# Making the scores of the dilated attention's next block between turning one block and multiplying another

## The chip, the cores and the metric

The kernel runs on one core of one Trainium2 chip. Its time is the device time of one execution in microseconds (us), the median of several runs. The engines are named as the profile names them: PE is TensorE (PEld its weight loads), DVE is VectorE, ACT is ScalarE, POOL is GpSimd, SP is SyncE. Each engine works through a queue of its own, and the queues meet only at semaphores.

## The reference, cut to what matters

The reference is two transformer blocks one after the other, on 1024 tokens of width 1024. The second block has four mixers side by side. Two of them matter here: an attention over dilated windows, and a state-space mixer called S5.

```python
DIL_PAIRS = ((128, 1), (512, 4), (2048, 16))      # window, dilation: three groups of four heads of 64

def dilated_group(q, k, v, bias_tab, window, dil):
    ...
    s = jnp.einsum('bdhnqe,bdhnke->bdhnqk', qb, kb, preferred_element_type=jnp.float32) / math.sqrt(E)
    s = jnp.where(mask[None, None, None], s + bias[None, None, :, None], -1e30)
    m = jnp.max(s, axis=-1, keepdims=True)
    p = jnp.exp(s - m)
    den = jnp.sum(p, axis=-1, keepdims=True)
    o = jnp.einsum('bdhnqk,bdhnke->bdhnqe', p, vb.astype(jnp.float32)) / den

def s5_mixer(u, a_re, a_im, log_dt, b_re, b_im, c_re, c_im, d_skip, w_glu):
    ...
    bu = jnp.einsum('gpc,bsgc->bsgp', b_bar, uf.astype(jnp.complex64))
    ...
    _, h = lax.associative_scan(combine, (a, bu), axis=1)
    ...
    y = jax.nn.gelu(y.reshape(B_, S_, S5_WIDTH))
    gl = y @ w_glu.astype(f32)
    y = gl[..., :S5_WIDTH] * jax.nn.sigmoid(gl[..., S5_WIDTH:])
```

## The kernel before, in words

The kernel is a sequence of stages with a barrier between them. The stage in question, `pool_and_dilated` (L3358), lies between 2298 and 2560 us of the span. It holds three kinds of work in one list of 45 steps: 6 steps of a pooling mixer, 28 of the dilated attention, 11 that mix its three groups. Every engine walks through the same steps, but each in its own time: the steps only fix the order inside each queue.

The attention has 24 blocks of 128 queries, 8 for each dilation, in the order 4, 16, 1. Block j is spread over several steps. Step 6 + j of each queue holds:

- PE: `scores(j)` (L3463; queries times keys for four heads, into two accumulator banks), `turn(j - 2)` (L3479; transposes the exponentials of block j - 2), `outputs(j - 3)` (L3489; turned exponentials times values).
- DVE: `largest(j)` (L3549; scales the scores and adds the bias, L3558, then takes maxima), `take_turned(j - 2)` (L3567), `output(j - 3)` (L3575, divides).
- ACT: `exps(j - 1)` (L3641), `take_turned(j - 2)` (L3650).

A block sees one or two parts of keys: with dilation 4 the odd blocks have two parts, with 16 all have one, with 1 all but the first have two. Two parts double the matmuls of a block. The profile counts each float32 matmul as two instructions, so `scores` shows as 8 or 16, `turn` as 4 or 8, `outputs` as 8 or 16.

Two waits tie these together. `scores(j)` waits for `scores_read`, which DVE raises in `largest(j - 1)` once it has read the two banks at L3558. `output(j - 3)` on DVE waits for `outputs(j - 3)` on PE.

After these pieces, each step appends others to the same queue. `turn_values` (L3415) transposes four blocks of values on PE; `take_values` (L3425, copy at L3435) empties them on DVE in even steps and on ACT in odd steps. Then one piece of the S5 core (class `S5Core`, L4277) may follow. Its four groups m are put at fixed steps:

```python
core = S5Core(c, io, s5, rooms, yT, (3, 7, 11, 15), (9, 13, 17, 21), (25, 28, 31, 34, 37, 40, 42, 44), u_loaded[1])
```

At steps 3, 7, 11, 15 PE runs `inputs(m)` (L4306); one step later DVE runs `turn(m)` (L4362), two steps later `scan(m)` (L4366 to L4373). POOL then makes the state from the scan (L4420). At steps 9, 13, 17, 21 PE runs `outputs(m)` of the core (L4319 and L4322, 48 instructions), called S5 outputs below. They wait for POOL's state, and for DVE having read the accumulators of the next group:

```python
            pe.wait_ge(self.s_ready, m + 1)
            pe.wait_ge(self.x_made, 4 * min(m + 2, 4))
```

When S5 outputs of group m are done, POOL issues the loads for group m + 1 (L4507, L4509), stores group m (L4439, after ACT's gelu, L4399), fetches the group before (L4444) and makes the state of group m + 1. From step 25 on PE runs eight gate products (L4336, two steps each), which read what POOL stored and fetched (`y_back`). ACT's sigmoid (L4406) and DVE's multiplication (L4380) follow each, and the next product waits for that multiplication.

Of the kernel before, what the change touches and what calls it, by code (L numbers as in the profile page):

```python
# [3357 lines left out]
def pool_and_dilated(c, io, proj, skewed, s5, rooms, heads, yT, spare, ident):  # L3358
# [3 lines left out]
    G, BLOCKS = len(POOLS), 3 * NB  # L3362
# [85 lines left out]
    def side_pe(pe):  # L3448
        for s in range(N_POOL):
            g = s - 1  # L3450
            if 0 <= g < G:
                if g == 0:
                    pe.wait_ge(pool_loaded, 32)
                pe.wait_ge(p_ready, g + 1)
                if g >= 2:
                    pe.wait_ge(p_out, g - 1)
                for n in range(2):
                    last = nc.tensor.matmul(c.ps[:, S0 + 2 * (g % 2) + n, :], wg[:, g, :], pooled[:, g % 2, n * BANK:(n + 1) * BANK],
                                            start=True, stop=True)
                last.then_inc(p_mixed, 1)  # L3460
            yield

        def scores(j):  # L3463
            n, b = divmod(j, NB)
            qk, (mine, prev) = qk_of[n], cuts[n][b]
            if j == 0:
                pe.wait_ge(p_out, G)
            else:
                pe.wait_ge(scores_read, j)
            if b == 0:  # L3470
                pe.wait_ge(qk_loaded[n], 16)
            for part in range(1 + prev):
                for h in range(DH):
                    r, t = slice(64 * (h % 2), 64 * (h % 2) + 64), h // 2
                    last = nc.tensor.matmul(c.ps[:, S0 + h % 2, (2 * part + t) * P:(2 * part + t + 1) * P], mine(qk[r, t, :]),
                                            cuts[n][b - part][0](qk[r, 2 + t, :]), start=True, stop=True)
            last.then_inc(scored, 1)

        def turn(j):  # L3479
            pe.wait_ge(exp_made, j + 1)  # L3480
            if j:
                pe.wait_ge(t_dve, j)
                pe.wait_ge(t_act, j)
            for part in range(parts_of(j)):
                for m in range(DH):
                    last = nc.tensor.transpose(c.ps[:, TR + part, m * P:(m + 1) * P], lg[j % 3][:, part, m * P:(m + 1) * P], ident[:, :])
            last.then_inc(turned, 1)

        def outputs(j):  # L3489
            n, b = divmod(j, NB)  # L3490
            parts, vd = parts_of(j), v_dil[:, n % 2]
            pe.wait_ge(t_dve, j + 1)
            pe.wait_ge(t_act, j + 1)
            if j:
                pe.wait_ge(o_made, j)
            if b == 0:
                pe.wait_ge(v_taken, (4, 8, 20)[n])
            for m in range(DH):
                h = 2 * (m % 2) + m // 2
                for part in range(parts):  # L3500
                    last = nc.tensor.matmul(c.ps[:, OB, h * DE:(h + 1) * DE], pt[:, j % 2, part, m * P:(m + 1) * P],
                                            vd[:, b - part, h * DE:(h + 1) * DE], start=(part == 0), stop=(part == parts - 1))
            last.then_inc(pv, 1)

        for j in range(N_DIL):
            if j < BLOCKS:
                scores(j)
            if 0 <= j - 2 < BLOCKS:
                turn(j - 2)
            if 0 <= j - 3 < BLOCKS:  # L3510
                outputs(j - 3)
            yield

        for s in range(N_MIX):
            b = s - 2
            if 0 <= b < NB:
                pe.wait_ge(y_ready, b + 1)
                for m in range(2):
                    last = nc.tensor.transpose(c.ps[:, S0 + 2 * m + b // 4, (b % 4) * P:(b % 4 + 1) * P], o[0][:, b, m * P:(m + 1) * P], ident[:, :])
                if b == NB - 1:  # L3520
                    last.then_inc(y_turned, 1)
            yield
# [214 lines left out]
    with nc.Block() as block:  # L3737
# [8 lines left out]
        @block.tensor  # L3746
        def _(pe):
            own = core.pe(pe)
            for step, _ in enumerate(side_pe(pe)):
                turn_values(pe, step)  # L3750
                next(own, None)
            for _ in own:
                pass
# [1027 lines left out]
```

## Time and profile before

| | us |
|---|---|
| median of 3 runs (3648.51 to 3652.16) | 3651.38 |
| profiled execution | 3652.57 |
| its span | 3650.8 |
| PE busy in the span | 3336.9 (91%) |
| DVE busy | 2105.9 (58%) |
| POOL busy | 1290.4 (35%) |

The profiled execution takes 1.77 us more than its span, and its time lies 1.19 us above the median. The shares are means over many stages with different limits. The rows further down therefore come from the one stage that the change touches; every time in them is counted from the start of the span.

### The profile page before, as it was taken

The page shows a single profiled execution, that of the slowest core. Times are in us where ns is not written, and L with a number is a line of the kernel's source. Part 1 is how long each engine was busy: PE and PEld are TensorE (multiplying, and loading weights), DVE is VectorE, ACT ScalarE, POOL GpSimd, SP SyncE. Part 2 cuts the span into 40 slices and gives each one's busy share as a digit, 9 for nine tenths or more (in the row PEclk, how much of TensorE's full clock was granted, in tenths as well). Part 3 has the DMA queues.
Part 4 walks back from the last instruction along what each step waited for, and adds up shares of the span by engine and source line. Part 5 has one row for each costly group of instructions (what it writes and reads, how often), then busy time and mean ns, then how long its engine had stood idle before and what let it go on. Part 6 is the DMA issues. An engine that isn't in the chain of part 4 may idle for free. (4 is left out here: it accounts for less than half of the span.)

```text
span 3650.8 us, 43830 instructions
## 1 busy us (share of the span) xinstructions
PE 3336.9 (91%) x16295; PEld 2663.9 (73%) x16295; DVE 2105.9 (58%) x3004; ACT 1306.3 (36%) x2270; POOL 1290.4 (35%) x1028
## 2 busy tenths in 40 slices
PE   5699999989899999969999999588889989999998
PEld 3577777776688888747888888375557768888887
DVE  5346664465876767883333333575555465555586
ACT  3523333143433334432223333153652233322344
POOL 4121212112655530145544454260435235544111
PEclk8799999889999999979999999799999999999999
DMA  8621112123233347224555332751025523333552
GB/s 255 221 61 46 51 57 90 49 99 110 70 116 101 101 140 241 75 70 134 115 113 121 116 116 93 203 164 64 31 67 152 167 93 101 98 104 101 199 183 98
DMA packets 357916, 418.46 MB, mean 115 GB/s; under 512 B 29798, under 2 KB 257586, under 8 KB 356282
## 3 DMA queue, kind: packets, MB, share of 16 engines
q1 hardware_dynamic: 350968, 391.84, 34.9%
q0 software_dynamic: 6016, 16.93, 1.9%
q10 hardware_dynamic: 722, 6.89, 0.5%
q8 instruction: 131, 2.15, 0.2%
q14 instruction: 79, 0.65, 0.1%
HBM read 294.06 MB, written 120.88 MB: 114 GB/s over the span
## 5 line engine op out<-in xcount | busy, mean ns | idle before, releaser
L2348 POOL TENSOR_TENSOR up_w_lo<-up_w_sum,up_w_hi 128x512 fp32r<-128x512 f32 x176 | 248.5, 1440 | 326.4 <-ACT up_w_hi L2324 324.5
L3282 POOL TENSOR_TENSOR px_w_lo<-px_w_sum,px_w_hi 128x512 fp32r<-128x512 f32 x140 | 204.8, 1493 | 281.4 <-ACT px_w_hi L3133 281.4
L2348 POOL TENSOR_TENSOR up_w_lo<-up_raw,up_w_hi 128x512 fp32r<-128x512 f32 x132 | 201.4, 1541 | 127.5 <-ACT up_w_hi L2324 127.5
L1924 ACT CAST down_hi<-down_room 128x1024 fp32r<-128x1024 f32 x154 | 161.0, 1051 | 210.7 <-PE ps L2204 137.1
L1928 DVE TENSOR_TENSOR down_lo<-down_room,down_hi 128x1024 fp32r<-128x1024 f32 x154 | 190.0, 1239 | 72.6 <-ACT down_hi L1924 71.4
L2324 ACT CAST up_w_hi<-up_w_sum 128x512 fp32r<-128x512 f32 x176 | 99.7, 614 | 323.5 <-DVE up_w_sum L2337 323.5
L766 PE MATMUL ps<-h_hi,stream_hi 128*128 128x512 f32 (+1 forms) x488 | 184.7, 378 | 24.5 <-POOL stream_lo L741 17.2
L2554 PE MATMUL ps<-h_hi_at,up_w_lo 128*128 128x512 f32 x704 | 191.3, 394 | 15.7 <-POOL up_w_lo L2348 15.7
L2554 PE MATMUL ps<-h_hi_at,up_w_hi 128*128 128x512 f32 x704 | 192.5, 396 | 8.0 <-ACT up_w_hi L2324 8.0
L3133 ACT CAST px_w_hi<-px_w_sum 128x512 fp32r<-128x512 f32 x140 | 79.9, 617 | 310.8 <-DVE px_w_sum L3213 310.8
L2554 PE MATMUL ps<-h_lo_at,up_w_hi 128*128 128x512 f32 x704 | 189.3, 391 | 0.0
L766 PE MATMUL ps<-h_hi,stream_lo 128*128 128x512 f32 (+1 forms) x488 | 184.7, 378 | 0.0
L766 PE MATMUL ps<-h_lo,stream_hi 128*128 128x512 f32 (+1 forms) x488 | 183.5, 376 | 0.0
L2166 POOL TENSOR_TENSOR down_room<-down_room 128x512 f32<-128x512 f32 x20 | 40.3, 2015 | 391.8 <-ACT down_room L1961 390.7
L3326 PE MATMUL ps<-xn_hi_at,px_w_hi 128*128 128x512 f32 x560 | 152.5, 395 | 23.7 <-ACT px_w_hi L3133 14.1
L2204 PE MATMUL ps<-down_hi 128*128 128x512 f32 x616 | 167.7, 394 | 3.4 <-ACT down_hi L1924 3.4
L2554 PEld LDWEIGHTS ps<-h_hi_at,up_w_lo 128*128 128x128 f32 x704 | 133.3, 190 | 45.2 <-POOL up_w_lo L2348 17.7
L2204 PE MATMUL ps<-down_hi,down_lo 128*128 128x512 f32 x616 | 165.3, 390 | 0.0
L2204 PE MATMUL ps<-down_lo,down_hi 128*128 128x512 f32 x616 | 164.7, 389 | 0.0
L3282 POOL TENSOR_TENSOR px_w_lo<-px_raw,px_w_hi 128x512 fp32r<-128x512 f32 x105 | 135.2, 1301 | 82.7 <-ACT px_w_hi L3133 82.7
L2554 PEld LDWEIGHTS ps<-h_hi_at,up_w_hi 128*128 128x128 f32 x704 | 134.1, 191 | 38.4 <-ACT up_w_hi L2324 9.7
L3326 PE MATMUL ps<-xn_hi_at,px_w_lo 128*128 128x512 f32 x560 | 151.2, 392 | 5.5 <-POOL px_w_lo L3282 5.5
(607 smaller groups left out, 8138.0 us busy)
## 6 DMA issues: line engine op xcount, KB each, us to landing
up_raw<-in_w_up SPq DMA_DIRECT2D x88, 512.0 KB, 4.2
down_room<-hid_kept SPq DMA_DIRECT2D x154, 256.0 KB, 2.9
hid_kept<-up_out SPq DMA_DIRECT2D x44, 512.0 KB, 3.6
down_room<-in_w_down SPq DMA_DIRECT2D x88, 256.0 KB, 4.3
px_raw<-in_w_in SPq DMA_DIRECT2D x38, 512.0 KB, 5.2
proj_kept<-xT SPq DMA_DIRECT2D x34, 512.0 KB, 6.0
px_raw<-in_w_gate SPq DMA_DIRECT2D x32, 512.0 KB, 5.2
gates_kept<-xT SPq DMA_DIRECT2D x32, 512.0 KB, 5.2
```

The costliest lines, as they stand in the source:

```text
L766: ins = nc.tensor.matmul(ps[:, self.bank + q % 2, 0:size], w[:, i % 2, k * P:(k + 1) * P], r[:, k, at:at + size], start=(x == 0), stop=(x ...
L1924: nc.scalar.copy(hi[:, u % R], both(u)).then_inc(hi_made, 1)
L1928: nc.vector.tensor_tensor(lo[:, u % R], both(u), hi[:, u % R].bitcast(F32), ALU.subtract).then_inc(rest_made, 1)
L2166: step(nc.gpsimd.tensor_tensor(total(half), sq(half, k - 1) if k == (H + 1 if half else 1) else total(half), sq(half, k), ALU.add))
L2204: ins = nc.tensor.matmul(bank(q, j), a[:, u % R, n, j * P:(j + 1) * P], b[:, u % R, 1 - n, :], start=(k == 0 and r == 0), stop=(k == KH - ...
L2324: nc.scalar.copy(w_hi[:, s, :], source(t, i)).then_inc(hi_made, 1)
L2348: nc.gpsimd.tensor_tensor(w_lo[:, s, :], source(t, i), w_hi[:, s, :].bitcast(F32), ALU.subtract).then_inc(lo_made, 1)
L2554: ins = nc.tensor.matmul(bank(t, i), wp[:, s, k * P:(k + 1) * P], op[:, k], start=(r == 0 and k == 0), stop=(r == 2 and k == H - 1))
L3133: nc.scalar.copy(self.w_hi[:, s, :], self.source(t, i)).then_inc(self.hi_made, 1)
L3282: nc.gpsimd.tensor_tensor(self.w_lo[:, s, :], self.source(t, i), self.w_hi[:, s, :].bitcast(F32), ALU.subtract).then_inc(self.lo_made, 1)
L3326: ins = nc.tensor.matmul(self.bank(t, i), wp[:, s, k * P:(k + 1) * P], op[:, k], start=(r == 0 and k == 0), stop=(r == 2 and k == H - 1))
```

## The change

PE makes the scores of a block one step earlier. Step 6 + j now holds `turn(j - 2)`, `scores(j + 1)`, `outputs(j - 3)`; step 6 also holds `scores(0)` ahead of that. The queues of DVE, ACT, POOL and SP keep their order, and no wait, buffer or size is changed.

```diff
@@ -3503,10 +3503,12 @@
             last.then_inc(pv, 1)
 
         for j in range(N_DIL):
-            if j < BLOCKS:
-                scores(j)
+            if j == 0:
+                scores(0)
             if 0 <= j - 2 < BLOCKS:
                 turn(j - 2)
+            if j + 1 < BLOCKS:
+                scores(j + 1)
             if 0 <= j - 3 < BLOCKS:
                 outputs(j - 3)
             yield
```

The order on PE in steps 8 and 9, up to the first S5 outputs, was as follows. L3475 is a matmul of `scores`, L3486 of `turn`, L3501 of `outputs`, L3422 of `turn_values`; the order counts each matmul once.

```order
L3475 MATMUL ps<-heads_21980 128x128 x8
L3486 MATMUL ps<-ident,xT 128x128 x8
L3501 MATMUL ps<-yT,xT 128x64 x4
L3422 MATMUL ps<-ident,dil_tokens_21984 128x128 x4
L4319 MATMUL ps<-s_chunk,s_room 128x128 x2
```

In the changed kernel the same place reads as follows; lines below the change are two higher (L4321 was L4319).

```order
L3475 MATMUL ps<-heads_21980 128x128 x8
L3422 MATMUL ps<-ident,dil_tokens_21984 128x128 x4
L3486 MATMUL ps<-ident,xT 128x128 x8
L3475 MATMUL ps<-heads_21980 128x128 x4
L3501 MATMUL ps<-yT,xT 128x64 x4
L3422 MATMUL ps<-ident,dil_tokens_21984 128x128 x4
L4321 MATMUL ps<-s_chunk,s_room 128x128 x2
```

The 8 matmuls of `scores(3)` are now ahead of the transposed values of step 8, and the 4 of `scores(4)`, which stood behind the S5 outputs, are ahead of them and of `outputs(0)`.

In steps 11 to 13, from the third `inputs` of the core (L4306) to the second S5 outputs, PE had this order.

```order
L4306 MATMUL ps<-s_chunk,s_bm 64x128 x16
L3475 MATMUL ps<-heads_21980 128x128 x4
L3486 MATMUL ps<-ident,xT 128x128 x4
L3501 MATMUL ps<-yT,xT 128x64 x8
L3422 MATMUL ps<-ident,dil_tokens_21984 128x128 x4
L3475 MATMUL ps<-heads_21980 128x128 x8
L3486 MATMUL ps<-ident,yT 128x128 x8
L3501 MATMUL ps<-yT,xT 128x64 x4
L3422 MATMUL ps<-ident,dil_tokens_21984 128x128 x4
L4319 MATMUL ps<-s_chunk,s_room 128x128 x2
```

Now it has this one.

```order
L4308 MATMUL ps<-s_chunk,s_bm 64x128 x16
L3486 MATMUL ps<-ident,xT 128x128 x4
L3475 MATMUL ps<-heads_21980 128x128 x8
L3501 MATMUL ps<-yT,xT 128x64 x8
L3422 MATMUL ps<-ident,dil_tokens_21984 128x128 x4
L3486 MATMUL ps<-ident,yT 128x128 x8
L3475 MATMUL ps<-dil_others 128x128 x4
L3501 MATMUL ps<-yT,xT 128x64 x4
L3422 MATMUL ps<-ident,dil_tokens_21984 128x128 x4
L4321 MATMUL ps<-s_chunk,s_room 128x128 x2
```

The scores of blocks 7 and 8 stand one step earlier, each between a `turn` and an `outputs`; those of block 8 (`dil_others`) have come to stand ahead of the second S5 outputs.

## Rows read from the trace of the kernel before

**Rows 1.** Stretches: us; busy PE, PEld, DVE, ACT, POOL; PEclk, DMA share, GB/s.

```profile
2369.50:2393.20 23.70, 23.67 (x216) 21.32 (x217) 21.21 (x43) 13.00 (x39) 17.16 (x24) 1.00 0.42 105
...
2466.90:2514.00 47.10, 45.08 (x273) 30.93 (x273) 21.88 (x42) 21.33 (x48) 1.49 (x2) 0.97 0.28 102
```

**Rows 2.** Who waited for `scores` (L3475): total us, times.

```profile
  DVE xT L3558: 19.0, 5
  DVE yT L3558: 10.1, 3
```

**Rows 3.** Timeline of PE, S5 outputs: start, us, work, [idle before <-releaser].

```profile
2369.53 0.68 PE L4319 MATMUL ps<-s_chunk,s_room 128*128 128x128 f32 x4 [0.46 <-DVE yT L4362]
...
2393.21 0.61 PE L4319 MATMUL ps<-s_chunk,s_room 128*128 128x128 f32 x4
...
2416.46 0.68 PE L4319 MATMUL ps<-s_chunk,s_room 128*128 128x128 f32 x4 [1.40 <-POOLq L4434]
...
2439.80 1.19 PE L4319 MATMUL ps<-s_chunk,s_room 128*128 128x128 f32 x4 [3.71 <-issue]
```

**Rows 4.** Timeline of POOL, one round of the S5 core.

```profile
2398.63 0.70 POOL L4507 DMA_DIRECT2D s_cp<-s_cp_scratch  x1 [4.36 <-PE ps L4322]
...
2415.05 1.26 POOL L4420 TENSOR_TENSOR s_room<-s_room,yT 128x512 f32<-128x512 f32 x1
```

**Rows 5.** Timeline of PE, steps 6 to 11 in part.

```profile
2355.86 1.12 PE L3422 MATMUL ps<-ident,dil_tokens 128*128 128x128 f32 x4 [7.68 <-DMA dil_tokens<-proj_kept]
2356.91 2.25 PE L3475 MATMUL ps<-heads 64*128 64x128 f32 x16
...
2364.53 2.24 PE L3475 MATMUL ps<-heads 64*128 64x128 f32 x16
2366.70 1.09 PE L3486 MATMUL ps<-ident,xT 128*128 128x128 f32 x8
2367.63 1.00 PE L3501 MATMUL ps<-yT,xT 128*128 128x64 f32 x8
2368.47 0.61 PE L3422 MATMUL ps<-ident,dil_tokens 128*128 128x128 f32 x4
...
2374.55 1.20 PE L3475 MATMUL ps<-heads 64*128 64x128 f32 x8
2375.68 0.66 PE L3486 MATMUL ps<-ident,yT 128*128 128x128 f32 x4
2376.17 1.90 PE L3501 MATMUL ps<-yT,xT 128*128 128x64 f32 x16
2377.91 0.61 PE L3422 MATMUL ps<-ident,dil_tokens 128*128 128x128 f32 x4
...
2382.92 1.97 PE L4306 MATMUL ps<-s_chunk,s_bm 128*64 128x128 f32 x32
```

**Rows 6.** Timeline of DVE, around step 6 and step 8.

```profile
2352.36 0.66 DVE L3558 SCALAR_TENSOR_TENSOR xT<-ps,dil_bias 128x512 f32<-128x512 f32 x1
...
2366.31 0.69 DVE L3435 COPY xT<-ps 128x512 f32<-128x512 f32 x1
2366.91 2.47 DVE L4362 TENSOR_TENSOR yT<-ps,s_cs 128x512 f32<-128x512 f32 x4
2369.30 1.41 DVE L3558 SCALAR_TENSOR_TENSOR xT<-ps,dil_bias 128x512 f32<-128x512 f32 x2
```

**Rows 7.** Timeline of PE, gate products after a wait and in full flow.

```profile
2466.93 5.15 PE L4336 MATMUL ps<-s_y_rows,s_cs 128*128 128x512 f32 x8 [3.81 <-DMA s_y_rows<-s_y_scratch]
...
2475.77 3.65 PE L4336 MATMUL ps<-s_y_rows,s_cs 128*128 128x512 f32 x8
```

**Rows 8.** Granted clock of PE (PEclk) around two waits: stretch, us, PE busy, PEclk.

```profile
2356.00:2358.00 2.00, 2.00 (x12) 0.50 0.02 6
...
2364.00:2366.00 2.00, 2.00 (x18) 1.00 0.86 238
...
2440.00:2442.00 2.00, 2.00 (x12) 0.50 0.00 1
```

## The prediction

> **What bounds the kernel now.** I read the stretches of the stage first. From 2369.5 to 2393.2 PE is busy for 23.67 of 23.70 us and DVE for 21.21 [rows 1], which looks like two full engines. The waits show the aim that such a change could have: DVE waits for `scores` at L3558 for 19.0 + 10.1 = 29.1 us, in 8 places [rows 2].
>
> What sets the end is shown by the timeline of the S5 outputs. They start at 2369.53, 2393.21, 2416.46 and 2439.80, that is 23.68, 23.25 and 23.34 us apart [rows 3]. The first was released by DVE's core `turn` (L4362), the third by POOL, and before the fourth PE idled for 3.71 us [rows 3]. Between two of them POOL has a full round: it starts 2398.63 - 2393.21 = 5.42 us after S5 outputs began, when they are done, and works until 2415.05 + 1.26 = 2416.31 [rows 4]. That is 17.68 us, and 0.15 us later PE starts the next ones [rows 3, 4]. So a round is at least 5.42 + 17.68 + 0.15 = 23.25 us, and the rounds of before are at that floor or 0.43 above it. After the fourth comes a chain through ACT, POOL and DMA to the first gate product at 2466.93, for which PE waits 3.81 us [rows 7]. From there to 2514 PE is busy 45.08 of 47.10 us [rows 1]. The stage thus ends by this chain: DVE turn, S5 outputs, four POOL rounds, gate products. An S5 output that starts late moves the end of the stage; waits of the attention beside it do not.
>
> **The change part by part.** No matmul is added or taken away; only PE's order changes. `scores(j + 1)` waits for DVE's read of block j (L3558), and now `outputs(j - 3)`, the values and the core's piece of the step are queued behind it. DVE in turn waits for those outputs and values before it goes on to the next read. So PE and DVE pass a baton in each step, where before the outputs, the values and the core's piece stood ahead of the waiting scores.
>
> The pieces, start to start unless said otherwise [rows 5]: scores 1.13 (8 instructions) and 2.17 (16), turn 0.49 (4) and 0.93 (8), outputs 0.84 (8) and 1.74 (16), values 0.61 busy, core inputs 1.97 busy; S5 outputs 2374.55 - 2369.53 = 5.02 [rows 3, 5]. On DVE [rows 6]: copy of values 0.60, core turn 2.39, read of a block 1.41 (two parts) or 0.66 (one). From DVE to PE 0.15: L4362 ends at 2369.38, PE starts at 2369.53 [rows 3, 6].
>
> *First S5 outputs.* Up to step 8 the change costs nothing: the values of step 6 still come by DMA at 2355.86 [rows 5]. From there 1.12 (values) + 0.60 (copy) + 1.41 (read of block 1) + 0.15 + 1.13 (scores 2) + 0.61 (values) + 1.97 (inputs) + 0.49 (turn) + 2.17 (scores 3) + 0.61 (values) + 0.60 (copy) leads to 2366.72, where DVE's core turn can start; it started at 2366.91 [rows 6]. I count that as equal. Then, however, PE needs the read of block 3 before it gets past `scores(4)`: 2369.30 + 1.41 + 0.15 = 2370.86 [rows 6], and behind it scores 1.13, outputs 0.84, values 0.61. S5 outputs start at 2373.44 in place of 2369.53: **+3.91**.
>
> *Second.* From the first: PE 5.02 + 0.49 + 2.17 (scores 5) + 1.74 + 0.61 = 10.03; DVE copy 0.60, read 1.41, 0.15 = 2.16; PE 1.13 (scores 6) + 0.84 + 0.61 + 1.97 (inputs) + 0.49 + 2.17 (scores 7) + 1.74 + 0.61 = 9.56; DVE copy 0.60, core turn 2.39, read 1.41, 0.15 = 4.55; PE 1.13 (scores 8) + 0.84 + 0.61 = 2.58. Together 28.88 against 23.68: **+5.20**. POOL's floor of 23.25 is covered.
>
> *Third.* PE 5.02 + 0.49 + 1.13 + 1.74 + 0.61 = 8.99; DVE 0.60 + 0.66 + 0.15 = 1.41; PE 1.13 + 0.84 + 0.61 + 1.97 + 0.49 + 1.13 + 1.74 = 7.91; DVE a division (no row; less than the 0.66 of twice the elements, taken as 0.4) + 2.39 + 0.66 + 0.15 = 3.60; PE 1.13 + 0.84 = 1.97. Together 23.88 against 23.25: **+0.63**.
>
> *Fourth.* Four steps without a core piece on PE; one such loop is 0.60 + 0.66 + 0.15 + 1.13 + 0.84 + 0.61 = 3.99, so 5.02 + 4 x 3.99 = 20.98, under POOL's floor: **0**. What hides the change here is POOL's round.
>
> *Behind it.* ACT's gelu of the last group stands behind its emptying of `turn(14)`, which no longer has 8 score instructions ahead of it on PE: at best **-1.1**. In the gate products PE is the bound; its idle time caps a gain at 47.10 - 45.08 = 2.0, and a two-part score in the wrong place (2.17) bounds a loss. I take 0.
>
> *The clock.* The baton makes PE idle before each of the first three S5 outputs: 3.60 to 4.55 us on DVE less the turn that PE can do meanwhile, so about 3.1 to 3.8. Waits of 3.81 and 3.71 us in before were followed by a granted clock of one half (1.2 GHz) [rows 3, 7, 8]: the gate product then took 5.15 in place of 3.65, 1.5 more [rows 7], and the first 4 S5 instructions 1.19 in place of 0.68 [rows 3]. Score matmuls lose nothing (2.25 for 16 at 0.50, 2.24 at 1.00 [rows 5, 8]). Per wait the price lies between 0 and 5.02 x 1.19 / 0.68 - 5.02 = 3.8. I take 1.0, the 1.5 of the gate product less what falls on the scores, three times: **+3.0**.
>
> Sum: 3.91 + 5.20 + 0.63 - 1.1 + 3.0 = +11.6 on the profiled execution (span 3650.8 and 1.77 around it, 3652.57): 3664.2. That execution lies 1.19 above the median, so 3663.0.
>
> **Rivals.**
>
> *Faster: DVE is the bound.* The first S5 outputs were released by DVE, not POOL [rows 3], and DVE is 89% busy in that round [rows 1]. If the 23.70 - 21.21 = 2.5 us that it idles per round were on the path, taking the waits for scores away would give 3 x 2.5, then 2.0 in the gate products and 1.1 at the gelu: 3651.38 - 10.6 = 3640.8. It decides as soon as PE gets through `scores(j + 1)` without a wait. Against it: two later rounds end on POOL, and the outputs that DVE needs now stand behind a read of its own.
>
> *Hardly a change: the floor holds.* DVE comes to its reads so early that the baton is hidden after the first round, and only POOL's floor counts: 3.91 - 0.43 - 1.1 = +2.4, 3653.8. For it: DVE starts its steps with nothing to wait for. Against it: the core's turn and the values copy lie between two reads.
>
> *No change: PE passes the waiting scores.* If what is behind them could overtake them, nothing would move: 3651.4. The row against it: at 2355.86 PE had idled 7.68 us for values, though `scores(1)` behind them had its read done at 2352.36 + 0.66 = 2353.02; it started at 2356.91, after the values [rows 5, 6]. The Trainium skill, "TensorE: Matmul & The Clock Gate", section "Architectural detail: the array is 16× 32×32, not 1× 128×128", says that PE's queue reorders only in part and can pull weight loads ahead of matmuls in flight. By that rule a matmul in wait still blocks those behind it, and the sum would stand; the trace agrees, with that 7.68.
>
> *Much slower: half clock in every S5 output.* 9.74 - 1.1 + 3 x 3.8 + 2 = +22, 3673.
>
> **How the numbers follow.** Forecast 0.67 (own range 3657 to 3671), much slower 0.14, floor 0.11, DVE bound 0.05, overtaking 0.03. A change under about 0.2% (7.3 us) cannot be told from none here. So slower takes the first two, 0.81; same takes floor and overtaking, 0.14; faster 0.05. The range 3654 to 3674 leaves out the DVE bound, overtaking, half of the floor and a little of the upper tail.
>
> **What would show it.** Right: S5 outputs (then L4321) 27 to 31 us apart from first to second, near 24 and 23.3 after; PE idle for 3 to 4 us at L3475 in front of each of the first three, released by DVE; DVE's waits at L3558 for scores mostly gone, new ones at L3580 for `outputs`; POOL waiting longer for PE. Wrong: rounds that stay at 23.3, or a stretch from the first gate product to the fourth much under 47 us.

## The result and the profile after

The changed kernel takes 3682.8 us (median of 4 runs, 3681.29 to 3688.69) against 3649.95 for the kernel before beside it: a ratio of 1.0093, 95% interval 1.0075 to 1.011. It is slower, as forecast, but by 33 us and not by 11.6, and the time lies above the range of 3654 to 3674. The profiled execution has a span of 3681.7 us (before 3650.8), PE's mean granted clock is 0.947 (before 0.955).

The chain that sets the end of the stage is the one that the prediction used, so I read the S5 outputs first. The timeline of PE in the changed kernel shows their starts (start, us, work), then the first gate product and one behind a late wait; L4321 was L4319, L4338 was L4336.

```profile
2377.03 1.06 PE L4321 MATMUL ps<-s_chunk,s_room 128*128 128x128 f32 x4
...
2415.87 1.06 PE L4321 MATMUL ps<-s_chunk,s_room 128*128 128x128 f32 x4
...
2443.07 1.17 PE L4321 MATMUL ps<-s_chunk,s_room 128*128 128x128 f32 x4
...
2470.53 1.13 PE L4321 MATMUL ps<-s_chunk,s_room 128*128 128x128 f32 x4
...
2494.91 3.65 PE L4338 MATMUL ps<-s_y_rows,s_cs 128*128 128x512 f32 x8
...
2512.72 1.16 PE L3475 MATMUL ps<-heads 64*128 64x128 f32 x16 [2.00 <-DVEq L3563]
2513.81 3.21 PE L3501 MATMUL ps<-yT,xT 128*128 128x64 f32 x16
2516.81 5.83 PE L4338 MATMUL ps<-s_y_rows,s_cs 128*128 128x512 f32 x8
```

The rounds are 38.84, 27.20 and 27.46 us, against 23.68, 23.25 and 23.34 in [rows 3]. None of these S5 outputs waits itself any more, and all four begin at 1.06 to 1.17 for the first four instructions, where three of before took 0.61 or 0.68.

The waits of the changed kernel, over its whole span (who waited for what: total us, times, longest), on PE and then on DVE:

```profile
PE ps L3475 <- DVEq L3563: 25.2, 13, 5.0
```

```profile
DVE dil_o L3582 <- PE ps L3501: 38.6, 21, 5.1
...
DVE xT L3574 <- PE ps L3486: 26.8, 10, 5.5
```

The row of the kernel before for the first of these two:

```profile
DVE dil_o L3580 <- PE ps L3501: 6.0, 3, 4.7
```

PE now waits before `scores` for DVE's read (L3563 is the signal behind it). DVE's 29.1 us of waiting for scores [rows 2] are gone, and in their place it waits 38.6 us for `outputs` (6.0 before) and 26.8 us for `turn` (2.7 before). That is the baton.

The second round of the changed kernel, on PE, from the wait ahead of the first S5 outputs to the one ahead of the second:

```profile
2368.41 1.04 PE L3486 MATMUL ps<-ident,xT 128*128 128x128 f32 x8
2373.18 1.30 PE L3475 MATMUL ps<-heads 64*128 64x128 f32 x8 [3.74 <-DVEq L3563]
2374.42 1.97 PE L3501 MATMUL ps<-yT,xT 128*128 128x64 f32 x8
2376.18 1.06 PE L3422 MATMUL ps<-ident,dil_tokens 128*128 128x128 f32 x4
...
2386.10 1.11 PE L3486 MATMUL ps<-ident,yT 128*128 128x128 f32 x4
2387.15 2.25 PE L3475 MATMUL ps<-heads 64*128 64x128 f32 x16
2389.33 3.67 PE L3501 MATMUL ps<-yT,xT 128*128 128x64 f32 x16
2392.79 1.06 PE L3422 MATMUL ps<-ident,dil_tokens 128*128 128x128 f32 x4
...
2396.02 1.30 PE L3475 MATMUL ps<-heads 64*128 64x128 f32 x8 [0.72 <-DVEq L3563]
...
2399.08 3.24 PE L4308 MATMUL ps<-s_chunk,s_bm 128*64 128x128 f32 x32
...
2412.01 1.33 PE L3475 MATMUL ps<-dil_others 64*128 64x128 f32 x8 [3.68 <-DVEq L3563]
2413.26 1.97 PE L3501 MATMUL ps<-yT,xT 128*128 128x64 f32 x8
2415.02 1.06 PE L3422 MATMUL ps<-ident,dil_tokens 128*128 128x128 f32 x4
```

The waits of 3.74 and 3.68 us are in the place and of the size foretold. What is larger is the work itself: 16 `outputs` take 3.67 where they took 1.90, values 1.06 for 0.61, the core's inputs 3.24 for 1.97 [rows 5]. These `scores` take the same 2.25. The granted clock of the same stretch (stretch: us, PE busy, PEclk, DMA share, GB/s) says why:

```profile
2368.00:2370.00 2.00, 1.44 (x12) 1.00 0.84 254
...
2376.00:2378.00 2.00, 2.00 (x10) 0.50 0.00 0
...
2392.00:2394.00 2.00, 2.00 (x11) 0.50 0.64 89
```

Before the wait PE ran at 2.4 GHz; behind it it was granted 1.2 GHz, and was still at that level in the stretch that begins 18.8 us after the wait's end, although PE was busy for 2.00 of 2.00 us in every such stretch from 2376 to 2394. The Trainium skill, "TensorE: Matmul & The Clock Gate", section "HAM oscillation — how this bites in real kernels", tells of a kernel whose waits for data between short bursts of matmuls bring the half clock back at every burst. The trace agrees with the repetition: half clock stands behind each of the waits of 3.74, 3.68 and, at 2440.05, 3.19 us.

Not all `scores` keep their time at half clock. The prediction read that from blocks with dilation 4, and it holds with dilation 16 as well (1.33 us for 8 at 2412.01, 1.32 at full clock at 2422.82). The blocks with dilation 1, behind the fourth S5 outputs, take 2.08 us where PEclk is 0.50 (2486 to 2488) and 1.16 where it is 1.00 (2498 to 2500):

```profile
2486.05 2.08 PE L3475 MATMUL ps<-heads 64*128 64x128 f32 x16 [0.83 <-DVEq L3563]
...
2499.37 1.16 PE L3475 MATMUL ps<-heads 64*128 64x128 f32 x16
```

### The profile page after: what moved, and what is told of

Read it like the earlier page. It is cut to its first block and busy times, and to the rows that moved or that the text cites. A ratio compares the mean times of both kernels' runs of the same rounds, so it can differ in the third digit from the quotient of the medians.

```text
span 3681.7 us, 43830 instructions
## 1 busy us (share of the span) xinstructions
PE 3368.0 (91%) x16295; PEld 2689.2 (73%) x16295; DVE 2106.2 (57%) x3004; ACT 1306.3 (35%) x2270; POOL 1289.5 (35%) x1028
## 5 line engine op out<-in xcount | busy, mean ns | idle before, releaser
L2554 PEld LDWEIGHTS ps<-h_hi_at,up_w_lo 128*128 128x128 f32 x704 | 133.6, 190 | 45.3 <-POOL up_w_lo L2348 17.7
```

The source lines that it names most:

```text
L2554: ins = nc.tensor.matmul(bank(t, i), wp[:, s, k * P:(k + 1) * P], op[:, k], start=(r == 0 and k == 0), stop=(r == 2 and k == H - 1))
```

## The experiments

The kernels differ only on PE, and in two cases on DVE. The table gives the ratio to the kernel before that ran beside each, and from the profiles the length of each stretch on PE: from `inputs(0)` to the first S5 outputs, the rounds to the second, third and fourth, from there to the first gate product, and from that to the fourth. The last column adds up these six stretches. The stretch from there to the last gate product is 36.76 or 36.77 in all but core_first (38.13), and is not in the sum. Where `inputs(0)` itself starts (2338.91 before, 2334.65 to 2346.43 in the others) hangs on a DMA ahead of the change and is left out too. Each kernel has one profile.

| kernel | ratio, 95% interval | to 1st | 2nd | 3rd | 4th | to gate | gate | sum against before |
|---|---|---|---|---|---|---|---|---|
| before | | 30.62 | 23.68 | 23.25 | 23.34 | 27.13 | 47.01 | |
| changed | 1.0093, 1.0075 to 1.011 | 36.84 | 38.84 | 27.20 | 27.46 | 24.38 | 49.59 | +29.3 |
| after_fill | 1.0044, 1.0028 to 1.0059 | 34.04 | 31.01 | 25.06 | 23.33 | 26.82 | 51.27 | +16.5 |
| late_at_core | 1.0036, 1.0026 to 1.0046 | 31.29 | 32.13 | 26.32 | 23.38 | 23.90 | 49.59 | +11.6 |
| core_first | 1.0092, 1.0075 to 1.0109 | 29.36 | 37.68 | 34.05 | 30.71 | 26.07 | 52.89 | +35.7 |
| before_fill | 1.0001, 0.9991 to 1.001 | 30.68 | 23.71 | 23.28 | 25.88 | 27.71 | 45.55 | +1.8 |
| early_to_step_9 | 1.0033, 1.002 to 1.0047 | 37.48 | 23.44 | 25.82 | 27.43 | 27.08 | 47.25 | +13.5 |
| early_from_step_22 | 1.0008, 0.9997 to 1.0018 | 29.94 | 23.67 | 23.26 | 26.07 | 28.25 | 49.57 | +5.7 |
| late_in_every_step | 1.0035, 1.0024 to 1.0047 | 36.41 | 32.60 | 24.03 | 27.44 | 25.54 | 45.63 | +16.6 |
| read_early_too | 1.0037, 1.0025 to 1.0049 | 34.88 | 30.14 | 23.31 | 26.19 | 26.16 | 45.91 | +11.6 |
| fill_two_waits | 1.0073, 1.0056 to 1.009 | 36.74 | 31.83 | 25.88 | 29.89 | 24.37 | 49.59 | +23.3 |
| read_early_and_fill | 1.0012, 1.0002 to 1.0022 | 35.47 | 27.40 | 23.81 | 23.34 | 22.36 | 47.26 | +4.6 |

My theory after the result: the waits are as forecast, and the half clock behind them, which slows everything on this path but the scores, is what I priced too low. The rival: the waits themselves are longer in sum than I worked out.

**after_fill: the waits filled with work.** PE turns the identity matrix into unused columns while it would wait, in steps 6, 7, 9, 13 and 17. The columns lie in the bank of the `outputs`, so from step 13 on the filling itself waits until DVE has divided the block that was there (`o_made`).

```diff
+        def keep_busy(n, j):
+            if n and j > 3:
+                pe.wait_ge(o_made, j - 3)
+            for _ in range(n):
+                nc.tensor.transpose(c.ps[:, OB, DH * DE:DH * DE + P], ident[:, :], ident[:, :])
...
+            keep_busy({0: 30, 1: 14, 3: 24, 7: 24, 11: 20}.get(j, 0), j)
             if j + 1 < BLOCKS:
                 scores(j + 1)
```

> The changed kernel with 112 extra transposes of the identity on PE (30, 14, 24, 24, 20), ahead of the early scores in steps 6, 7, 9, 13 and 17, where PE idled 4.95, 2.16, 3.74, 3.68 and 3.19 us. They write columns that nothing reads. Clock theory: most of the loss is half clock after these waits; with PE kept at work the first S5 outputs come 4 to 5 us late, the next 28 to 30 us after, the next about 24, and the time is 3655 to 3665. Baton theory alone (the order costs all 33 us, the clock little): 3678 to 3690, rounds of 36 to 39 us as in the changed kernel.

Measured 3669.84, between the two: 16.05 us over the kernel before beside it (3653.79), where the changed kernel was 32.85 over its own. The timeline of PE around the first S5 outputs and the starts of the others:

```profile
2368.73 2.78 PE L3509 MATMUL ps<-ident 128*128 128x128 f32 x24
2372.64 1.30 PE L3475 MATMUL ps<-heads 64*128 64x128 f32 x8 [1.12 <-DVEq L3570]
...
2375.26 0.61 PE L4328 MATMUL ps<-s_chunk,s_room 128*128 128x128 f32 x4
...
2406.27 0.61 PE L4328 MATMUL ps<-s_chunk,s_room 128*128 128x128 f32 x4
```

The wait for DVE is as long as in the changed kernel (2.78 of filling and 1.12, for 3.74), and yet the S5 outputs run at full clock. What is left is nearly the prediction's sum without its clock: +3.42, +7.33, +1.81, -0.01 for the four rounds where it had +3.91, +5.20, +0.63, 0. Of the 7.33, 1.71 is a short stretch still at half clock around 2391, behind a wait of 1.29: `inputs` 2.68 to the next start (1.90 before), `outputs` 1.31 (0.84) and values 0.99 (0.53).

**fill_two_waits: only the two longest.** As above with `{3: 24, 7: 24}`.

> The changed kernel with 24 extra transposes of the identity (about 2.8 us at full clock, into unused columns) ahead of the early scores in steps 9 and 13 alone, where TensorE waited 3.74 and 3.68 us. The waits on VectorE stay. If the half clock behind these two waits is the larger part of what I missed, S5 outputs of chunk 0 and 1 take 5 us in place of 9.1 and 6.4 and the pieces behind them their full-clock times: 8 to 13 us less than the changed kernel, 3670 to 3676 (changed kernel 3683). If the clock follows these waits only a little, 3679 or more.

Measured 3679.14, at the lower end of the second case; by its interval the ratio can't be told from that of the changed kernel. The trace has 6.0 us less: 7.0 in the second round (31.83 for 38.84) and 1.3 in the third, against 2.4 more in the fourth. The first is as late as there. Its pieces in front of the filling and behind it:

```profile
2361.51 3.31 PE L4315 MATMUL ps<-s_chunk,s_bm 128*64 128x128 f32 x32
...
2374.02 1.51 PE L3501 MATMUL ps<-yT,xT 128*128 128x64 f32 x8
...
2376.18 1.06 PE L4328 MATMUL ps<-s_chunk,s_room 128*128 128x128 f32 x4
```

The inputs already ran at half clock (3.31), behind the waits in steps 6 and 7 which after_fill also filled; and behind the filled wait the half clock came all the same, only for a shorter time. after_fill had the same filling here and the same 1.12 us of waiting left, and kept full clock. So the waits in steps 6 and 7 may count too; one profile of each kernel does not show it.

**late_at_core: the scores at the end of the four steps with S5 outputs.**

```diff
-            if j + 1 < BLOCKS:
+            if j + 1 < BLOCKS and N_POOL + j not in core.at_out:
                 scores(j + 1)
             if 0 <= j - 3 < BLOCKS:
                 outputs(j - 3)
             yield
+            if j + 1 < BLOCKS and N_POOL + j in core.at_out:
+                scores(j + 1)
```

> The changed kernel, except that in the four steps with S5 outputs (9, 13, 17, 21) the scores of the next block stand last, behind the S5 outputs. If the loss comes from S5 outputs standing behind a wait for DVE: first S5 outputs at the place of before (within 1.5 us), rounds of about 26, 23.3 and 23.3, time 3650 to 3658. If early scores cost in every step, because DVE waits for the outputs behind them: 3664 or more.

Measured 3666.59, on the second side. The first S5 outputs are back in place (31.29), all four run at full clock, and still the second round takes 32.13: PE waits for DVE in the plain steps between them, and the 16 `outputs` behind such a wait run at half clock:

```profile
2379.90 2.25 PE L3475 MATMUL ps<-heads 64*128 64x128 f32 x16 [1.76 <-DVEq L3565]
2382.08 3.68 PE L3501 MATMUL ps<-yT,xT 128*128 128x64 f32 x16
```

So early scores cost in every step, not only where S5 outputs stand behind them.

**core_first: the core's piece ahead of the early scores.**

```diff
             if 0 <= j - 2 < BLOCKS:
                 turn(j - 2)
+            yield
             if j + 1 < BLOCKS:
                 scores(j + 1)
```

At the new `yield` PE appends the core's piece of the step; the values follow at the end.

> The changed kernel with the core's piece (inputs, S5 outputs, gate products) put between turn and the early scores in every step of the attention, the values behind outputs. Scores stay early. If the S5 outputs behind the waiting scores are the cause: rounds of 23.3 to 26, time 3647 to 3657. If early scores cost in every step: 3664 or more. A gate product ahead of outputs could also hold up DVE late in the stage, by 2 to 4 us.

Measured 3688.14, on the second side, and by its ratio as slow as the changed kernel. The S5 outputs no longer stand behind the wait for the read, but the first three stand behind one of 2.39 to 2.63 us for the core's turn and fall to half clock. `outputs` and scores now stand behind 5.6 to 8.0 us of S5 outputs. DVE's timeline and then PE's, in the second round:

```profile
2380.18 0.42 DVE L3583 TENSOR_TENSOR dil_o<-ps,dil_stat 128x256 f32<-128x256 f32 x1 [6.44 <-PE ps L3501]
...
2381.72 2.63 DVE L4385 TENSOR_TENSOR_SCAN yT<-vec,yT 128x128 f32<-128x128 f32 x8
2384.26 0.67 DVE L3561 SCALAR_TENSOR_TENSOR xT<-ps,dil_bias 128x512 f32<-128x512 f32 x1
```

```profile
2385.04 2.25 PE L3475 MATMUL ps<-heads 64*128 64x128 f32 x16 [4.10 <-DVEq L3564]
2387.22 3.67 PE L3501 MATMUL ps<-yT,xT 128*128 128x64 f32 x16
```

DVE waits 6.44 us for outputs, then owes the core its scan (L4378 to L4385) before it reads the next scores; PE waits 4.10 us for that read. The baton passes twice in the step.

**early_to_step_9: only the first wait.**

```diff
-            if j < BLOCKS:
+            if j == 0 or 5 <= j < BLOCKS:
                 scores(j)
             if 0 <= j - 2 < BLOCKS:
                 turn(j - 2)
+            if j <= 3:
+                scores(j + 1)
```

> Scores one step early in steps 6 to 9 only, up to the first S5 outputs; from step 10 on the order of before. My prediction's own terms for this part: +3.91 us of waiting before the first S5 outputs and +1.0 for the clock behind it, so about 3655 (before at about 3650), S5 outputs of chunk 0 in about 6 us. If the half clock after the one wait of 3.7 us is what I mis-sized, the outputs of chunk 0 take about 9 us, the scores' neighbours behind them (turn, outputs, values) also run at half clock until about 17 us after the wait, and the time is 3661 to 3667.

Measured 3665.43. The time is that of the second case, but not for its reason. Up to the first S5 outputs this kernel and the changed one have the same order, and both wait 3.74 us. Here the granted clock behind that wait was:

```profile
2374.00:2376.00 2.00, 2.00 (x12) 0.50 0.00 0
2376.00:2378.00 2.00, 2.00 (x20) 0.90 0.83 262
2378.00:2380.00 2.00, 2.00 (x22) 1.00 0.00 0
```

Half clock ended about 5 us after the wait (which ended at 2371.38) in place of about 22, and the S5 outputs took 2380.63 - 2374.91 = 5.72, not 9.07. The first round has the loss (+6.86); the third and fourth, in the order of before, lose 2.57 and 4.09 more: in the third the core's inputs wait 2.59 us for a load (0.97 before), and the fourth is long because the third S5 outputs fell to half clock again (9.05).

**early_from_step_22: only the gate stretch.**

```diff
-            if j < BLOCKS:
+            if j <= 16:
                 scores(j)
             if 0 <= j - 2 < BLOCKS:
                 turn(j - 2)
+            if 16 <= j < BLOCKS - 1:
+                scores(j + 1)
```

> The order of before up to step 21, scores one step early only from step 22 on, that is in the gate stretch. My prediction has 0 (within 2 us) for this part: 3648 to 3652, first gate product to fourth 47 us apart. From the changed kernel's trace, where this stretch took 2.6 us longer, a gate product behind a 2.0 us wait at half clock: 3652 to 3656, 49.6 us.

Measured 3656.41 against 3653.45, a ratio that cannot be told from 1. Its trace has the 49.57 of the second case, with the same wait of 2.00 us and a slow gate product behind it (5.41; 5.83 in the changed kernel), so about +2.6 belongs to this stretch; the runs neither confirm nor exclude it. The trace shows something else. Its third S5 outputs, still in the order of before, start as in [rows 3] behind a wait for POOL, of 1.39 us here and 1.40 there:

```profile
2416.88 0.68 PE L4321 MATMUL ps<-s_chunk,s_room 128*128 128x128 f32 x4 [1.39 <-POOLq L4436]
...
2418.13 0.89 PE L4321 MATMUL ps<-s_chunk,s_room 128*128 128x128 f32 x4
2418.96 1.23 PE L4324 MATMUL ps<-s_room,s_cp 64*128 64x127 f32 x8
```

Here the clock falls in the middle of them; in the profiled execution of before it did not. POOL's round then ends later, and the fourth takes 26.07 in place of 23.34.

**before_fill: the clock in the kernel before.** 24 such transposes ahead of the fourth S5 outputs and of the first gate product, in the order of before.

```diff
-            pe.wait_ge(self.out_loaded[m], 16 * (S5_L + 1))
-            pe.wait_ge(self.s_ready, m + 1)
...
+                keep_busy(24)
+            pe.wait_ge(self.out_loaded[m], 16 * (S5_L + 1))
+            pe.wait_ge(self.s_ready, m + 1)
...
+                    keep_busy(24)
+                    pe.wait_ge(self.y_back, 16 * 4)
```

> The kernel before with 24 extra transposes on PE ahead of the fourth S5 outputs and 24 ahead of the first gate product, after the waits that are over and before the last one (POOL's state, the fetch). Its waits there were 3.71 and 3.81 us, each followed by half clock. Clock theory: S5 outputs take 5.0 in place of 9.1 and the gate product 3.65 in place of 5.15, time 3644 to 3647. If the clock does not follow these waits: 3650 to 3652.

Measured 3654.61 against 3653.79: no change that can be told, and neither case. The first gate product took 3.70 in place of 5.15, as intended, which alone is too little for the time to show. The fourth S5 outputs did not: after 2.78 us of filling PE still waited 2.96 us for POOL and ran at half clock; and the third fell to it behind 1.42 us, as above, which cost 2.54 in the next round.

**late_in_every_step: the scores behind the outputs.** I took the loop to be closed by DVE's division, which needs the `outputs` that stand behind the waiting scores.

```diff
             if 0 <= j - 3 < BLOCKS:
                 outputs(j - 3)
+            if j + 1 < BLOCKS:
+                scores(j + 1)
```

> Scores of the next block last in every step (turn, outputs, scores, then values and core piece). They still pass the values and the core piece, but the outputs no longer stand behind them, so VectorE's division of the outputs, which stands before its next read, no longer waits for the scores that wait for that read. If this loop is the cause: no wait over 1 us for VectorE before scores, S5 outputs 23 to 25 us apart, 3647 to 3655. If scores ahead of the values and the core piece cost by themselves (as the rows of late_at_core would also allow): 3660 or more.

Measured 3666.28; this theory falls. Up to the fourth S5 outputs DVE now waits 4.2 us for `outputs` (21.9 in the changed kernel), but PE still waits ahead of the S5 outputs:

```profile
2373.73 1.31 PE L3475 MATMUL ps<-heads 64*128 64x128 f32 x8 [2.90 <-DVEq L3563]
```

```profile
2369.82 2.47 DVE L4364 TENSOR_TENSOR yT<-ps,s_cs 128x512 f32<-128x512 f32 x4
2372.22 1.40 DVE L3560 SCALAR_TENSOR_TENSOR xT<-ps,dil_bias 128x512 f32<-128x512 f32 x2
```

The read (L3560) that the scores need stands behind the core's turn (L4364), as the prediction had it, and not only behind the division. The wait is shorter by the 0.84 of `outputs` that PE does meanwhile.

**read_early_too: DVE one block ahead as well.**

```diff
+            if j == 0:
+                largest(0)
             if 0 <= j - 2 < BLOCKS:
                 take_turned(j - 2)
+            if j + 1 < BLOCKS:
+                largest(j + 1)
             if 0 <= j - 3 < BLOCKS:
                 output(j - 3)
```

> The changed kernel, and VectorE too makes its part of block j+1 one step early: it copies the turned block, then reads the scores of the next block, and only then divides the outputs. The read that TensorE's scores wait for is then not behind the division any more. If the loop through the division is the cause of the waits: TensorE's waits before scores fall from 25 us in 13 to under 5, no long stretch at half clock, 3645 to 3655, at best a little faster than before. If VectorE's work itself is the bound in these steps, or the core's piece on VectorE holds the reads up as before: 3660 or more.

Measured 3665.29, in the second case. The waits ahead of scores did go all the same:

```profile
PE ps L3475 <- DVEq L3563: 6.1, 5, 5.0
```

(5.0 of it is ahead of `scores(1)`, in step 6.) But the core's turn now stands behind that early read, so the S5 outputs wait for the turn, and the clock falls there:

```profile
2369.53 0.86 PE L4323 MATMUL ps<-s_chunk,s_room 128*128 128x128 f32 x4 [1.82 <-DVE yT L4366]
2370.33 1.23 PE L4326 MATMUL ps<-s_room,s_cp 64*128 64x127 f32 x8
```

These S5 outputs take 2378.40 - 2369.53 = 8.87 us. So the core's piece on DVE still holds PE up, as the second case has it, but ahead of the S5 outputs and no longer ahead of the scores.

**read_early_and_fill: both.** The kernel before this one with the filling, `{3: 14, 7: 12, 11: 16, 15: 24}`.

> The kernel in which VectorE reads one block early as well, and 14, 12, 16 and 24 extra transposes (about 1.6 to 2.8 us) ahead of the early scores in steps 9, 13, 17 and 21, where TensorE still waited 1.4 to 4.6 us before S5 outputs. If what was left there (about 12 us over before) is the half clock: 3650 to 3657, S5 outputs all in about 5 us. If it is work that now stands in another order: 3662 or more.

Measured 3658.78 against 3655.73, ratio 1.0012, in the first case's reach but for 2 us:

```profile
2381.90 0.68 PE L4330 MATMUL ps<-s_chunk,s_room 128*128 128x128 f32 x4 [0.85 <-DVE yT L4373]
...
2387.02 0.65 PE L3486 MATMUL ps<-ident,yT 128*128 128x128 f32 x4
```

The S5 outputs all run at full clock (2387.02 - 2381.90 = 5.12 us for the first). With both edits, the 29.3 us of loss in the trace become 4.6. More than that is left of the loss itself: +4.85 and +3.72 stand in the first two rounds, and 4.77 is given back ahead of the first gate product, 3.95 of it because the fourth S5 outputs run at full clock (5.11 us) where before they took 9.06. The profiled execution is the slowest of ten. No kernel here is faster than the one before, and no round in the table is under POOL's floor of 23.25 us.

## Why the prediction was right in direction and wrong in size

- **The chain, right.** The end is set by DVE's turn, S5 outputs and POOL's rounds. PE's waits ahead of the first three S5 outputs were 3.74, 3.68 and 3.19 us, foretold as 3.1 to 3.8. DVE's waits for scores became waits for outputs.
- **First, +3.91: measured +6.22.** Start to start, `outputs` took 1.76 in place of 0.84, values 0.85 in place of 0.61 and inputs 2.73 in place of 2.13 at half clock: 1.76 together. What is left, 4.46, is 0.55 over the term.
- **Second, +5.20: measured +15.16.** The pieces on the path that ran at half clock, start to start against before: S5 outputs 9.07 - 5.02 = 4.05, turn 0.56, two `outputs` 1.72 + 0.92, inputs 1.20, three values 1.09. Together 9.54, and 5.62 is left for the baton.
- **Third, +0.63: measured +3.95.** S5 outputs 6.36 - 5.02 = 1.34 and `outputs` 0.92 are clock. 1.69 is left, 1.06 over the term: every stretch of the sum came out 0.1 to 0.4 longer.
- **Fourth, 0: measured +4.12.** It is POOL's floor, as I said; but POOL's round begins when S5 outputs are done, and these took 9.17, 4.15 more than at full clock. 23.25 + 4.15 = 27.40 against 27.46. after_fill, with full clock there, has 23.33. PE's own queue came to these S5 outputs at the same time: POOL was done at 2470.33, and PE started at 2470.53 without idling. In fill_two_waits it came later: PEclk was 0.50 for the whole round, POOL was done at 2461.17 and PE started at 2463.78, a round of 29.89. So the sum of 20.98 for PE, which was to lie under the floor, does not hold at half clock.
- **Behind it, -1.1: measured -2.75.** Of this, 2.68 is that the fourth S5 outputs took 6.38 and not the 9.06 of before. Of the gelu's 1.1, 0.80 shows (POOL's store starts 3.40 us after the S5 outputs' end, before 4.20), but PE itself then came to the first gate product without waiting for the loads, with `outputs`, `turn` and scores ahead of it in part at half clock.
- **The gate stretch, 0 within 2.17: measured +2.58.** It is just outside my bounds: 2.00 us of waiting, 2.18 on one gate product and 1.16 on the `outputs` ahead of it, less 1.50 that the first gate product no longer loses and 1.09 for scores that now stand ahead of the stretch, together 2.75.
- **The clock, +3.0: the step that failed.** I charged 1.0 for each of three waits, worked out from one gate product, and bounded each by S5 outputs at half clock alone (3.8). Measured on the path are 1.76 + 9.54 + 2.26 + 4.15 = 17.7 us, less the 2.68 given back behind the fourth. Two things were left out. The half clock lay on most of what stands on the path between the S5 outputs as well; of that only `scores` keep their time, and not even they do with dilation 1, against what I read from two rows. And S5 outputs at half clock raise POOL's floor, so that the fourth round, where I had put nothing, lost as well. The 3.8 was no bound for S5 outputs alone either: they lost 4.05 and 4.15. The rounds' baton comes to 4.46 + 5.62 + 1.69 = 11.8 where I had 9.74.
- **The rivals.** DVE as the bound and the hidden baton are out, since PE's waits are there. So is overtaking: `outputs` never started ahead of the waiting scores in the rows above. "Much slower" was the nearest, but it took the clock for the S5 outputs alone and reached 3673.

The experiments show both parts. In the four rounds the changed kernel loses 29.45 us and after_fill, with the waits kept and PE kept busy, 12.55, of which 1.71 is still half clock: 10.84 is left where I had 9.74. With PE's waits at the scores taken away (read_early_too) the sum of the table falls from 29.3 to 11.6, but part of the half clock goes with them, so the two shares overlap; with both edits it is 4.6. The medians against the kernel before beside each agree: 32.85, 16.05 (after_fill), 11.84 (read_early_too) and 3.05 (both).

Two things stay open. Why half clock stayed so much longer in one kernel than in another with the same order and the same wait ahead of it was not settled. And each sum rests on one profile, while profiles of the same order differ by 2.5 to 2.7 us in one round, as shown below.

## What to carry to other kernels

A wait put into PE's queue cost here its length and what followed at the lower clock, and that was not one instruction: price every piece on the path up to the next stretch that the trace shows at full clock, at its rate at 1.2 GHz. Where another engine's round starts at the end of such a piece, its floor moves too. Before moving work ahead across a step, ask which read must come first, and what stands ahead of that read on its own engine: moving the producer alone only turned the consumer's wait into the producer's here.

## What the hardware showed that I had not expected

- Behind the same wait of 3.74 us in the same order, half clock ended about 5 us after the wait in one execution and about 22 us after it in another, PE being busy without a gap for 20 us in both.
- Behind waits of 1.39 and 1.42 us for POOL the clock fell in two profiled executions with the order of before up to there, and behind one of 1.40 us in a third it did not [rows 3]. The round that follows differs by 2.5 to 2.7 us, so one profile of before does not tell its clock.
- 2.78 us of filling did not hold the clock across the 2.96 us of waiting that followed it.
- `scores` of dilations 4 and 16 take the same time at both clocks, those of dilation 1 take 2.08 us at half and 1.16 at full.
